# A decoder step on one core: cached pages and sample rows issued by SyncE too, retention norms on token quarters, fillers and splits moved

## The reference

```python
# even layer: retention and a spatial-gating MLP, one input and one output projection
q, k, v, g, u, sv = split(rms_norm(x) @ e_w_in, 6)
o, s1   = retention(rope(q), rope(k) * dk**-0.5, v, s0)      # 4 heads of 128
ret_out = silu(g) * rms_unit(o)                              # norm over the 128 of a head
svn     = layer_norm(sv)                                     # 4 groups of 128
x += rms_norm(concat(ret_out, u * gate(svn)) @ e_w_out)
x += rms_norm(conv_ffn(rms_norm(x)))                         # GLU with a causal conv of width 3

# odd layer: native sparse attention, 16 heads of 64, 4 kv heads
q, rows_c, rows_s, rows_w, gates = project(rms_norm(x) @ o_w_in)
kc, vc = compress(rows_c of the prompt, or cached pages + new rows of a sample)
o = gates[0] * cmp_attend(q, kc, vc) + gates[1] * sel_attend(q, rows_s) + gates[2] * window_attend(q, rows_w)
x += rms_norm(o @ o_w_out)
x += rms_norm(conv_ffn(rms_norm(x)))
```

## Time and profile before

| | |
|---|---|
| median of 3 runs | 1677.16 us (1674.13 to 1679.83) |
| the profiled execution | 1678.8 us |
| its span, first to last instruction | 1677.0 us |
| mean granted TensorE clock | 0.979 |
| DVE, ACT, POOL busy | 48%, 41%, 13% of the span |
| DMA | 138.49 MB, 83 GB/s on average |

### The profile page before, as it was taken

The page is one execution under the profiler, slowest core; times in us unless marked ns, Lnnn a source line. Parts: engine busy times, 40 slices in busy tenths (PEclk is TensorE's granted clock), DMA queues, the critical chain, the costliest instruction groups (busy, mean ns, idle before and its releaser), DMA issues.

```text
span 1677.0 us, 31572 instructions
## 1 busy us (share of the span) xinstructions
PE 1599.6 (95%) x13167; PEld 1452.4 (87%) x13167; DVE 807.6 (48%) x1326; ACT 680.1 (41%) x1301; POOL 219.0 (13%) x582
## 2 busy tenths in 40 slices
PE   8999989899999999999998899997999999999996
PEld 6899978599999999998898566565989999999995
DVE  5755452455531555336333476753165552255523
ACT  3122134354532555324321466654335552255522
POOL 3000001200000000001013245432001000000000
PEclk9999999999999999999999699999999999999998
DMA  6312226123233232331335300013312223323231
GB/s 217 101 53 76 101 84 173 39 56 95 67 92 109 76 86 75 92 93 52 109 104 114 145 8 2 1 57 98 84 51 72 79 74 94 101 75 100 60 83 54
DMA packets 185561, 138.49 MB, mean 83 GB/s; under 512 B 11376, under 2 KB 177504, under 8 KB 185392
## 3 DMA queue, kind: packets, MB, share of 16 engines
q1 hardware_dynamic: 175536, 106.31, 22.2%
q0 software_dynamic: 9920, 30.74, 6.0%
HBM read 128.21 MB, written 13.01 MB: 84 GB/s over the span
## 4 chain that ended last, share of the span: by engine, by line
PE 71%; DVE 4%; issue 2%; ACT 2%; POOLq 1%; POOL 1%; DMA 1%; SPq 0%; DVEq 0%; ACTq 0%
PE gemm L944 41%; PE gemm L603 10%; PE gemm L614 6%; PE misc L578 4%; PE gemm L1086 2%; PE misc L1117 2%; POOLq L509 1%; PE misc L700 1%; PE misc L676 1%; DMA raw<-in_o_w_out 1%; PE gemm L662 1%; DVE y L1660 1%; PE gemm L1081 1%; PE misc L1111 1%; PE misc L691 0%
## 5 line engine op out<-in xcount | busy, mean ns | idle before, releaser
L1626 DVE TENSOR_TENSOR wL<-raw,wH 128x2048 fp32r<-128x2048 f32 (+2 forms) x107 | 222.1, 2076 | 227.1 <-ACT wH L1259 227.0
L944 PE MATMUL gemm<-hH,wH 128*128 128x272 f32 x1280 | 268.5, 291 | 0.3 <-DVE wL L1626 0.2
L944 PE MATMUL gemm<-hH,wL 128*128 128x272 f32 x1280 | 264.8, 288 | 0.0
L944 PE MATMUL gemm<-hL,wH 128*128 128x272 f32 x1280 | 264.0, 288 | 0.0
L1259 ACT ACTIVATE wH<-raw 128x2048 fp32r<-128x2048 f32 (+2 forms) x107 | 185.2, 1731 | 55.2 <-PE gemm L603 32.7
L944 PEld LDWEIGHTS gemm<-hH,wH 128*128 128x128 f32 x1280 | 200.5, 188 | 6.5 <-issue 5.2
L944 PEld LDWEIGHTS gemm<-hL,wH 128*128 128x128 f32 x1280 | 201.0, 188 | 0.0
L944 PEld LDWEIGHTS gemm<-hH,wL 128*128 128x128 f32 x1280 | 199.9, 189 | 0.0
L1883 DVE SCALAR_TENSOR_TENSOR conv<-up,rows_t,conv 128x560 f32<-128x560 f32 x88 | 70.6, 802 | 211.8 <-ACT conv L1259 211.8
L614 PE MATMUL gemm<-wH,hH 128*128 128x256 f32 x448 | 130.0, 290 | 13.2 <-ACT qN L1259 4.2
L603 PE MATMUL gemm<-hH,wH 128*128 128x272 f32 (+1 forms) x624 | 133.5, 295 | 4.3 <-DVE hL L2078 2.5
(11 more groups left out here) (364 smaller groups left out, 2862.4 us busy)
## 6 DMA issues: line engine op xcount, KB each, us to landing
raw<-in_f_w_in SPq DMA_DIRECT2D x88, 512.0 KB, 5.0
raw<-in_f_w_out SPq DMA_DIRECT2D x32, 704.0 KB, 4.5
raw<-in_e_w_in SPq DMA_DIRECT2D x12, 1024.0 KB, 5.2
raw<-in_o_w_in SPq DMA_DIRECT2D x10, 1024.0 KB, 5.2
raw<-in_e_w_out SPq DMA_DIRECT2D x4, 1024.0 KB, 5.3
pages<-in_cache_cmp POOLq DMA_DIRECT2D x16, 256.0 KB, 3.6
raw<-in_o_w_out SPq DMA_DIRECT2D x16, 256.0 KB, 5.8
rows<-in_cache_sel POOLq DMA_DIRECT2D x12, 256.0 KB, 2.8
```

The source lines that it names most:

```text
L944: ins = pe.matmul(gemm[odd][:, n, 0:TH], w, x[:, k, n * TH:(n + 1) * TH], start=(k == 0 and part == 0), stop=(k == nk - 1 and part == 2))
L1626: order(dve.tensor_tensor(unit_view(wL, u), unit_view(raw, u), unit_view(wH, u).bitcast(F32), ALU.subtract), lo_ready)
```

## The change

It has these parts:

1. SP waits for x before the first weight unit, and PE does 20 fillers for 14.
2. DVE takes the sample's rows of unit `E_IN + 3` inside `layer_norm`, ahead of the last token tile.
3. The heads' norms lie with token quarter q on partitions 32q to 32q+31 (head h in row h of them, `mean_k` is then [128, heads, 32] with one column set), so root and reciprocal have 136 columns, and a quarter of a head is spread by a broadcast column of the identity.
4. `load_page` is shared: SP issues the odd pages up to 11, POOL the even ones and 12 to 15.
5. ACT's copies to `cPT` come four at a time after each token tile of n == 4.
6. `split_hi` and `split_lo` of the first o_w_out unit come after the loop over o_w_in. ACT loads the table for Exp ahead of the attention, by one small Exp, and takes turned rows in ahead of the exps. PE gets 3 fillers before each of the turns 2 to 5 and 4 before each of the first four units.
7. SP loads the rows of samples 0, 1, 2, 4, 6, POOL those of 3, 5, 7; sample 2's go to a weight slot that is free (`raw`, slot `O_OUT % 2`), and the load of weight unit `O_OUT + 2` moves behind sample 3's output.
8. PE gets 16 fillers after the second FFN and 5 after each of the first six m; the y stores are issued by SP.

```diff
-        mean_d, mean_k = sb("mean_d", [P, 32]), sb("mean_k", [P, 32])
+        mean_d, mean_k = sb("mean_d", [P, 32]), sb("mean_k", [P, RH, 32])
...
-        row_slot = [rows0[:, 0], rows0[:, 1], rows1[:, 0], rows1[:, 1]]
+        row_slots = [rows0[:, 0], rows0[:, 1], rows1[:, 0], rows1[:, 1]]
+        spare = raw[:, O_OUT % 2, :].rearrange("p (e q c) -> p e q c", e=2, q=NPG)
+        row_slot = [rows0[:, 0], rows0[:, 1], spare] + [row_slots[(b - 1) % 4] for b in range(3, DB)]
...
+        def load_page(eng, n, landed_sem):
+
+            if n >= 4:
+                eng.wait_ge(paired, n // 2 - 1)
+            page = eng.value_load(a["page_table"][n // NPG:n // NPG + 1, n % NPG:n % NPG + 1], min_val=0, max_val=N_POOL - 1)
+            eng.dma_start(pages[64 * (n % 2):64 * (n % 2) + 64, (n // 2) % 2],
+                          a["cache_cmp"][0, page].rearrange("(t l) z g d -> t l z g d", l=2)).then_inc(landed_sem, 16)
...
+            sp.wait_ge(x_in, 48)
             for u in range(F0):
                 if u == E_OUT + 3:
                     sp.wait_ge(phase, 2 * N_BAR)
+                    for n in range(1, 4, 2):
+                        load_page(sp, n, page_sp[n // 2 % 2])
                     for z, phi in enumerate((phiK, phiV)):
                         src = a[("o_phi_k", "o_phi_v")[z]][0].rearrange("(t l) d e -> l d t e", l=2)
                         for l in range(2):
                             sp.dma_start(phi[64 * l:64 * l + 64, :, :], src[l]).then_inc(phi_in, 16)
                 load_unit(u)
+            for n in range(5, 12, 2):
+                load_page(sp, n, page_sp[n // 2 % 2])
             load_ffn(0)
-            for u in range(O_IN, O_OUT + 3):
+            for u in range(O_IN, O_OUT + 2):
                 load_unit(u)
...
+            sp.wait_ge(lo_ready, O_OUT + 1)
+            load_rows(sp, 2, row_first[2])
+            sp.wait_ge(ks_turned, 2)
+            load_rows(sp, 4, row_first[0])
+            sp.wait_ge(os_done, 2)
+            load_rows(sp, 6, row_first[1])
+            sp.wait_ge(os_done, 3)
+            load_unit(O_OUT + 2)
             load_unit(O_OUT + 3)
             load_ffn(1)
+            for m0, m1 in ((0, 4), (4, 7), (7, 8)):
+                sp.wait_ge(out_ev, 2 * m1)
+                cols = slice(m0 * P, m1 * P)
+                sp.dma_start(o["y_prompt"][0].rearrange("(t p) d -> p t d", p=P)[:, :, cols], yout[:, 1:NT, cols]).then_inc(out_stored, 16)
+                sp.dma_start(o["y_sample"].rearrange("b s d -> (b s) d")[:, cols], yout[0:NS, 0, cols]).then_inc(out_stored, 16)
+            sp.wait_ge(out_stored, 96)
...
-            stay_busy(14)
+            stay_busy(20)
...
-                for n in range(2):
-                    ins = pe.matmul(gemm[last % 2][32 * h:32 * h + 32, n, 0:TH], mean_k[:, :], hsqs[h % 2][:, n * TH:(n + 1) * TH],
-                                    start=True, stop=True)
+                for q in range(4):
+                    ins = pe.matmul(gemm[last % 2][32 * q:32 * q + 32, 0, 0:TQ], mean_k[:, h, :], hsqs[h % 2][:, q * TQ:(q + 1) * TQ],
+                                    start=(h == 0), stop=(h == RH - 1))
...
-                for n in range(2):
-                    ins = pe.matmul(misc[:, 2 * (h % 2) + n, 0:TH], spread[:, h, :], kT[:, 1, n * TH:(n + 1) * TH], start=True, stop=True)
+                for q in range(4):
+                    ins = pe.matmul(misc[:, 2 * (h % 2) + q // 2, (q % 2) * TQ:(q % 2 + 1) * TQ],
+                                    ident[:, 32 * q + h:32 * q + h + 1].to_broadcast([P, P]), kT[:, 1, 0:TQ], start=True, stop=True)
...
+                if n >= 2:
+                    stay_busy(3, b5)
                 turn_in(n)
             for n in range(N_UNITS + LAG + 1):
+                if n < LAG:
+                    stay_busy(4, b5)
                 if LAG <= n < N_UNITS + LAG:
...
+            stay_busy(16, gemm[0][:, 0, :])
...
+                if m < DC - 2:
+                    stay_busy(5, gemm[0][:, 0, :])
...
-            activate(halves(kT[:, 0, :]), gemm[(FIRST_CHUNK[E_OUT] - 1) % 2][:, :, 0:TH], ACT.Sqrt, hroot, bias=eps[:, 0:1])
+            activate(kT[:, 0, 0:TQ], gemm[(FIRST_CHUNK[E_OUT] - 1) % 2][:, 0, 0:TQ], ACT.Sqrt, hroot, bias=eps[:, 0:1])
...
+            def take_rows_turned(z):
+                act.wait_ge(cp_turned, z + 1)
+                for g2 in range(2):
+                    tokens = misc[64 * g2:64 * g2 + 64, z, :].rearrange("p (u s l) -> p l s u", s=8, l=2)
+                    for l in range(2):
+                        activate(cPT[64 * l:64 * l + 64, z // 2, :, g2, z % 2, :], tokens[:, l, :, :], ACT.Copy, cp_ev if g2 and l else None)
...
-                split_hi(u + 1)
+                if n < 10:
+                    split_hi(u + 1)
...
-                if n == 3:
-                    for z in range(4):
-                        act.wait_ge(cp_turned, z + 1)
-                        for g2 in range(2):
-                            tokens = misc[64 * g2:64 * g2 + 64, z, :].rearrange("p (u s l) -> p l s u", s=8, l=2)
-                            for l in range(2):
-                                activate(cPT[64 * l:64 * l + 64, z // 2, :, g2, z % 2, :], tokens[:, l, :, :], ACT.Copy, cp_ev if g2 and l else None)
-                elif n in (5, 7):
+                    if n == 4:
+                        take_rows_turned(t - 1)
...
+            split_hi(O_OUT)
...
+            activate(root_probe[:, :], eps[:, 0:1], ACT.Exp)
...
+                if 1 <= n < 7 and n % 2:
+                    take_in(5 + n)
                 if 1 <= n <= N_UNITS:
                     exps(n - 1)
-                if 1 <= n < 7 and n % 2:
-                    take_in(5 + n)
...
+                    if t == NT - 1:
+                        sample_rows(E_IN + 3, vN[0:NS, 0, 256:512])
...
-                    sample_rows(u, vN[0:NS, 0, 256:512])
...
-            order(dve.reciprocal(kT[:, 1, :], kT[:, 0, :]), hrec)
+            order(dve.reciprocal(kT[:, 1, 0:TQ], kT[:, 0, 0:TQ]), hrec)
...
+                            if b < 6:
+                                dve.wait_ge(page_in[b % 2], 16 * (b // 2 + 1))
+                                dve.wait_ge(page_sp[b % 2], 16 * (b // 2 + 1))
+                            else:
+                                dve.wait_ge(page_in[b % 2], 80)
...
-                split_lo(u + 1)
+                if n < 10:
+                    split_lo(u + 1)
...
+            split_lo(O_OUT)
...
-            for n in range(6):
-                load_page(n)
+            for n in range(0, 4, 2):
+                load_page(pool, n, page_in[n // 2 % 2])
             for z in range(2):
                 pool.dma_start(pe_in[:, z, :], a[("o_pe_k", "o_pe_v")[z]][0].rearrange("(t l) d -> t (l d)", l=2)).then_inc(pe_in_land, 16)
-            for n in range(6, DB * NPG):
-                load_page(n)
+            for n in (4, 6, 8, 10, 12, 13, 14, 15):
+                load_page(pool, n, page_in[n // 2 % 2])
...
-                if b + 2 < DB:
-                    if b >= 2:
-                        pool.wait_ge(os_done, b - 1)
-                    load_rows(pool, b + 2, row_in[(b + 2) % 4])
+                if b in (0, 2, 4):
+                    if b:
+                        pool.wait_ge(os_done, (1, 4)[b // 2 - 1])
+                    load_rows(pool, b + 3, row_in[b // 2])
```

More of the change, by code:

```diff
@@ L369, in build_program @@
         xt_turned, xt_ready, gain_ready = sem("xt_turned"), sem("xt_ready"), sem("gain_ready")
-        phi_in, page_in = sem("phi_in"), [sem(f"page_in{n}") for n in range(4)]
+        phi_in, page_in = sem("phi_in"), [sem(f"page_in{n}") for n in range(2)]
         page_turned, page_ev, pe_in_land = sem("page_turned"), sem("page_ev"), sem("pe_in_land")
@@ L693, in spread_rstd, with stay_busy @@
                 order(ins, rstd_ready)
-            def stay_busy(count):
+            def stay_busy(count, bank=None):
                 for _ in range(count):
-                    pe.matmul(b7[:, 0:P], ident[:, :], ident[:, :], start=True, stop=True)
+                    pe.matmul((b7 if bank is None else bank)[:, 0:P], ident[:, :], ident[:, :], start=True, stop=True)
             pe.wait_ge(ident_in, 16)
-            stay_busy(14)
+            stay_busy(20)
             pe.wait_ge(x_in, 48)
@@ L1165, in rows_turn @@
                         for pg in range(NPG):
-                            ins = turn(misc[:, br, (2 * j + pg) * P:(2 * j + pg + 1) * P], row_slot[b % 4][:, br, pg, j * P:(j + 1) * P])
+                            ins = turn(misc[:, br, (2 * j + pg) * P:(2 * j + pg + 1) * P], row_slot[b][:, br, pg, j * P:(j + 1) * P])
                     order(ins, ks_turned)
@@ L1866, in project_out @@
                         for b in PAIRED_AT[i]:
-                            for n in (2 * b, 2 * b + 1):
-                                dve.wait_ge(page_in[n % 4], 16 * (n // 4 + 1))
+                            if b < 6:
[3 more added lines that the diff above has]
```

(5 more changed lines are left out.)

32 lines of the change are left out of this document (12 added, 20 removed).

## The result

The changed kernel takes 1657.88 us (median of four runs, 1655.7 to 1661.26), the kernel before 1675.64 in the same comparison: a ratio of 0.9894, 95% interval 0.9865 to 0.9923. In a second comparison it was 1656.9 against 1680.2, a ratio of 0.9867 (0.9846 to 0.9888). The profiled executions, from which all that follows is read, are 1678.8 and 1657.72 us (spans 1677.0 and 1655.9): 21.1 us. The forecast was 28.0, to 1650.8, with a range from 1637 to 1664.

The account below looks back on a forecast made before the run. PE was taken as the bound, busy 1599.6 of 1677.0 us, so gains lie at its waits and half clock. Terms -2.3 - 2.5 - 1.7 - 4.5 - 5.3 - 11.5 - 3.5 + 3.3 = -28.0 from 1678.8 gave 1650.8; range 1637 to 1664.

Parts of the forecast that it names:

- the fillers do not hold the clock: Rival at the attention's start: first groups stay at 0.50, gain 3.5 instead of 11.5, total 1658.8; chance 0.20.
- 4.2 + 2.8: Attention start: PE's 4.2 us wait for q, and 2.8 us of slow matmuls behind it, both go.
- 2.3 + 1.2: Attention start, costs: 2.3 us for DVE's low half ahead of the taking in, 1.2 charged for the new fillers.
- the clock's 11.0: Attention start, 934 to 961 us: full clock saves 11.0, taken as 8 because DVE and ACT set part of the pace.
- The rival was right in its mechanism: Cached pages: FFN weights come late behind SP's pages, their -4.5 becomes +1, total 1656.3; chance 0.10.
- the one I set at 1.1: Cached pages: price of the FFN's first weights queued behind page 11 on SP, 1.1 us, between 0 and 5.0.
- its term, +1.4: Samples: new DVE wait for POOL's mask copy of sample 5, behind loads awaiting sample 3's output; costs +1.4 us.
- half of it lies beside PE's work: Samples: only half of the new mask wait, sized by the nearest row at 2.88 us, costs PE time: +1.4.
- x without weights beside it should land a little before 10.8: Opening: loading x ahead of the weights brings it slightly before 10.8 us, part of the -2.3 gain.
- the rival of +0.9: Opening: the fillers miss x, +0.9 for -2.3, total 1654; chance 0.04.
- 1.7 + 4.3 - 1.0 = 5.0: Closing filler cost: first output turn 1.7 late, six longer steps +4.3, turns shortened at full clock -1.0.
- The rival that the clock falls in the later groups: Attention, 961 to 1022 us: scattered fillers end, groups run at 1.2 GHz, +48, total 1707; chance 0.03.

Follow-up runs that it names:

- the split alone: The kernel before with only the first o_w_out unit's split moved behind the o_w_in loop, no fillers or early table load: 1674.91 us against 1680.2.
- the low half at unit 40: The changed kernel with VectorE's low-half split of the first o_w_out unit moved from ahead of the attention to the 40th score unit: 1660.37 us.
- the second trace: The changed kernel itself, unedited, run and traced again beside the mended kernel on the same chip: 1656.9 us.
- the first fence: Trace excerpt of the closing in the changed kernel, fillers kept, shown beside one of the run without closing fillers; profiled execution 1657.72 us.

## Why the prediction was right in sign and too large in size

**What bounds.** That the gains are at PE's single waits and at the stretch of half clock held: -12.8, -5.3 and -2.8 of the shift lie at three of the places named, and the chain is PE's for 89%. The total, 1657.9, lies inside the range and beside the 1658.8 of the rival "the fillers do not hold the clock", but that is chance: the attention gained more than forecast, and the pages, samples, norms and opening gave nothing.

**Sample rows, turned cached rows.** -2.8 and -5.3 for -2.5 and -5.3. Both waits went, nothing took their place, and the half clock behind the second went with it.

**Start of the attention.** -12.8 for -11.5. The total held; the working held in part. The wait and its half clock gave 7.0 as summed (4.2 + 2.8); what was given back was 5.1 and not 2.3 + 1.2; and of the clock's 11.0 all came, where I took 8. Of the 5.1, 2.2 are the low half, as charged. The other 2.9 are not shown to be the fillers': without them PE kept its distance through the first turns (2.4 us at 905 and at 914) and waited longer for DVE's qT (2.85 for 2.04), and the split alone, with no filler, gave back 4.7. What I had wrong is who did it: I laid it on the fillers and gave "the fillers do not hold the clock" the second-largest chance. With no filler at all the moved split gave 9.5. The rule of the Trainium skill ("TensorE: Matmul & The Clock Gate", Part 4), that a transpose does not count as busy for the clock in the same way, does not decide here: in the kernel with the split alone the same transposes without fillers saw the clock rise after 17 us and not 27, and with the low half at unit 40 the turns were 6.25 of PE's 16.14 busy us in the 17 us ahead of 1011, at 1.00, and 6.05 of 17.00 in the 17 behind, at 0.50. On the table load, the Trainium skill ("ScalarE: Activation LUTs", What ACT_TABLE_LOAD costs) adds a drain to the 1.28; the trace has the load 0.02 us behind ACT's instruction before it and the next function 1.30 us after the load's start, so the measurement decides for 1.28.

**Pages.** -0.3 for -4.5. The rival was right in its mechanism: the FFN's weights behind SP's pages. The term that was mis-sized is the one I set at 1.1 (bounds 0 to 5.0): it cost 5.8 us of shift between 284 and 290 (a wait of 6.67, with half clock around it). I had noted that the weights stand behind page 11 and had the landing, 5.0; I had not put a time on the issue, which came 17 us later than before, and they were there 8 us after it, with pages and the next unit's weights beside them. A page also took SP 2.9 to 3.1 us from issue to issue, and not at most 2.6. With the weights in front, the part gave 3.8.

**Samples.** +1.2 for -3.5. The four waits on rows went, and the new wait was named and placed rightly; its term, +1.4, was mis-sized. I took the nearest row, 2.88, and half of it; it was 5.12, and the half clock behind it brought the price to 4.3. The step that failed is "half of it lies beside PE's work": POOL's loads wait for sample 3's output, a whole sample step later than what that row stood behind.

**Norms.** -0.1 for -1.7. The terms came as summed or better (0.99 for the reciprocal, no wait, the spread 4.02 and not the 0.4 slower). What failed is the silence on the clock: a stretch of 6.8 us at 0.50 ahead of the spread cost the same 2.2.

**Opening.** +0.6 for -2.3, and -1.4 in the second trace: which of the two comes is luck, as far as these runs show. Two steps failed in both. "x without weights beside it should land a little before 10.8": it came at 11.44 and 11.09, and with the weights beside it at 11.09. And the fillers did not take 0.44 each: the clock rose under them, 20 took 6.25 and 7.14 us, and they ended 2.4 and 1.2 us ahead of x. In the first trace the rival of +0.9 had the size.

**Closing.** +0.1 for +3.3. The fillers cost 3.2 against 1.7 + 4.3 - 1.0 = 5.0: the first turn came 1.2 late and not 1.7, and the steps were 1.67 and not 2.0, since the rows of turns and fillers overlap (in the first fence the fillers start 0.55 behind turns that last 0.71). The stores on SP gave 3.1 and not 1.7, because the end behind the last issue got shorter too, not only the issues. That the two nearly cancel is luck; the forecast had them at +5.0 and -1.7.

**Slower.** The rival that the clock falls in the later groups did not come in the changed kernel. That it can was seen with the low half at unit 40, 17 us at 0.50 for 6.4 us.

## What to carry to other kernels

When work is moved to an idle queue, put a time on the first thing behind it in that queue, and on when its reader wants it: both losses of this change, 5.8 and 4.3 us, were a load with a wait in front of something that another engine needed soon. Order them so that the urgent one goes first: here the two orders gave 3.5 and 4.3 us in single runs, and together with three smaller edits 12 us. On a PE-bound kernel price a stall with the half clock that can follow it, and remove the stall before adding fillers: here moving one split gave 9.5 us, the fillers at most 2.0, and those at the end cost 3. And when a part of the sum hangs on half clock, look at more than one trace of the same kernel before explaining it.

## What the runs showed of the hardware

- PE can stay at half clock for long although it is busy all the while: 17.00 of 17 us at 0.50 in the middle of the attention, 6.4 us of time, when a VectorE instruction of 2.29 us was put there and PE waited 0.86. Waits of 0.73 and 1.47 us elsewhere in that loop were not followed by one; what decides is open.
- The same six stores end the program 2.5 us after their last issue from SP's queue and 5.7 us after it from POOL's.
- A unit of 1 MB in two issues (one of 512 KB lands in 5.0 us at the median) took 8 us from the first issue to use when pages from two queues and the next unit's weights were beside it.
- Loading x first, without weights beside it, did not bring it sooner: PE began to turn it at 10.74 to 11.44 us in nine traces with this order and 20 fillers, at 11.09 without it, and at 10.80 in the kernel before. In the trace of the changed kernel GpSimd's loads of constants run beside it.
